# Sixteen ring slots, the first two experts' loads first, and single row buffers in a mixture-of-experts stage on one core

## The chip, the cores and the metric

The kernel runs on one core of a Trainium2 chip. The metric is the device time of one execution in microseconds (us); lower is better. TensorE does the matrix products, VectorE (DVE) and ScalarE (ACT) work on elements, GpSimd (POOL) does small work and issues the row gathers and scatters, and SyncE (SP) issues the weight loads. Sixteen DMA engines move the data for all queues.

## The reference

One layer of a diffusion backbone on 640 tokens (128 context, 512 latent) of 1024 channels, in float32: attention and merge, then a mixture of experts. Only the last part matters here:

```python
D_MODEL, N_GROUPS, EXPERTS_PER_GROUP, TOP_K, D_EXPERT = 1024, 4, 8, 2, 512     # 32 experts
g_sel = argmax(t @ w_router_group + b_router_group)                  # one group of 4 per token
le_sel = (t @ w_router_expert + b_router_expert) of that group       # 8 logits
top_v, top_i = top_k(le_sel, 2)
w_pair = softmax(group logits)[g_sel] * softmax(top_v)
for each expert e: hb = silu(x @ w1[e]) * (x @ w3[e]);  y = (hb @ w2[e]) * weight
channel_sublayer(x) = x + gate * rms_norm(sum of the two experts' y, g_post_ffn)
```

w1 and w3 of an expert are 1024 x 512, w2 is 512 x 1024: 2 MiB each, so that the 32 experts are 192 MiB. A token goes to two experts.

## The kernel before

**Stages.** Projections, attention, merge and the output product take the first 575 us. Then the rows `h2` are normed, stored to a scratch tensor `h2_d` (5 stores of 0.5 MiB on SyncE's queue), and the router follows. Its end is a chain of small VectorE operations: logits, one-hots, positions of each token in its expert's list, the slot table (which token stands in which of an expert's 128 slots: `tab_g` for gathers, `tab_s` for scatters), then the experts' ranks by size and their numbers in that order (`expert_ids`). 

**Passes.** 18 passes process 1, 2 or 4 experts together (`WIDTHS`). The first two (`LEAD`) take experts 0 and 1 by number, the others take experts by rank. A pass gathers its 128 rows by an indirect DMA (`gather`, L968 to L977), TensorE transposes them (`transpose_x`), ScalarE copies the columns, and then come the products with w1 and w3 (`up`), the gate on ScalarE and VectorE, and w2 (`down`). The result is copied to `ysb` (`y_half`) and scattered to `y_d` (`scatter`). Gathered rows (`xg`) and results (`ysb`) have two buffers each, taken in turn. The last pass isn't scattered; its rows are added on chip. At the end five pair loads of 1 MiB bring `y_d` back, and the final rows are made from them and from x1, which stays on chip (`xrow`).

**Units and loads.** `expert_units` cuts each pass into 6 units (w1, w3 and w2 in two halves each). A unit reads one load of 1 MiB for each expert of its pass. The order of units is that of TensorE; the order of loads is that of SyncE. In the prediction a unit or load is called by its number, from 0:

| unit | what | loads before |
|---|---|---|
| 0, 1 | pass 0, w1 | 0, 1 |
| 2, 3 | pass 0, w3 | 2, 3 |
| 4, 5 | pass 1, w1 | 4, 5 |
| 6, 7 | pass 0, w2 | 6, 7 |
| 8, 9 | pass 1, w3 | 8, 9 |
| 10, 11 | pass 2, w1 (two experts) | 10 to 13 |
| 12, 13 | pass 1, w2 | 14, 15 |
| 14, 15 | pass 2, w3 (two experts) | 16 to 19 |
| 16, 17 | pass 3, w1 (four experts) | 20 to 27 |
| 18, 19 | pass 2, w2 (two experts) | 28 to 31 |
| 20, 21 | pass 3, w3 (four experts) | 32 to 39 |

Load j goes to ring slot j % 15. SyncE issues strictly in order, and load j waits for the unit of load j - 15 (`ring_load`, L731 to L742):

```python
if j >= RING:
    sp.wait_ge(moe_mm, moe_loads[j - RING][0] + 1)
```

Loads 0 to 2 go out as the last raw weight slots come free, 3 to 8 as the last split weights do, 9 after the `h2` stores, 10 to 14 after the expert numbers; 13 waits for the first gather as well (L758). Slots 9 to 14 (`rows_ring`) lie where the merged rows and modulation rows were. The order on GpSimd's queue is: gathers 0 and 1, two loads of gate rows, the store of the pair weights, then for each pass the gather two passes on, and the scatter.

Of the kernel before, what the change touches and what calls it, by code (L numbers as in the profile page):

```python
# [7 lines left out]
ALU = mybir.AluOpType  # L8
# [9 lines left out]
P = 128  # L18
# [19 lines left out]
RAW_MIX, RING, HL = 3, 15, 3  # L38
# [70 lines left out]

def build(nc, t):  # L110
# [16 lines left out]
    with ExitStack() as ctx:  # L127
# [32 lines left out]
        h2T = at("h2T", D, offset=att_base + (NT + 6) * D * 4)  # L160
        assert att_base + (NT + 7) * D * 4 <= att_end
# [66 lines left out]
        xg = at("expert_rows", 2 * D, offset=late_base + 2 * D * 4)  # L228
        ysb = at("expert_y", 2 * D, offset=late_base + 4 * D * 4)
        gT = at("expert_g_columns", FE, offset=late_base + 6 * D * 4)  # L230
        g2_rows = at("last_gate_rows", D, offset=late_base + 6 * D * 4 + FE * 4)
# [4 lines left out]
        rows_ring = at("rows_ring", (RING - RAW_MIX - 2 * HL) * UNIT, offset=att_base)  # L236
        assert att_base + (RING - RAW_MIX - 2 * HL) * UNIT * 4 <= att_end
# [28 lines left out]
        rbase = [late_base + 4 * D * 4]  # L266

        def rb(name, cols, dt=F32):
            a = at(name, cols, dt, offset=rbase[0])
            rbase[0] += (cols * (2 if dt == BF16 else 4) + 31) // 32 * 32  # L270
            assert rbase[0] <= late_base + 6 * D * 4
            return a

        kbase = [late_base + 7 * D * 4 + FE * 4]

        def kept(name, cols, dt=F32):
            a = at(name, cols, dt, offset=kbase[0])
            kbase[0] += (cols * (2 if dt == BF16 else 4) + 31) // 32 * 32
            assert kbase[0] <= late_base + 2 * KD * TOK * 4
            return a  # L280
# [50 lines left out]
        def ring(slot):  # L331
# [5 lines left out]
            x = slot - RAW_MIX - 2 * HL  # L337
# [352 lines left out]
        def _(sp):  # L690
# [40 lines left out]
            def ring_load(j):  # L731
# [5 lines left out]
                if p == NP:  # L737
                    if u == 0:
                        sp.wait_ge(all_scattered, 1)
                    load_pair(u)  # L740
# [54 lines left out]
        def _(po):  # L795
# [172 lines left out]
            def gather(p):  # L968
                if p >= 2:
                    po.wait_ge(moe_xt, p - 1)  # L970
# [4 lines left out]
                po.indirect_dma_start(out=xg[:, par * D:(par + 1) * D], out_offset=None, in_=h2_d,  # L975
# [3 lines left out]
            def scatter(p):  # L979
# [5 lines left out]
                                      in_=ysb[:, par * D:(par + 1) * D], in_offset=None,  # L985
# [13 lines left out]
            gather(1)  # L999
# [5 lines left out]
            po.dma_start(wk_d.rearrange("(t p k) o -> p t (k o)", p=P, k=2), wk[:, :].rearrange("p (t k) -> p t k", k=2)).then_inc(g2_in, 16)  # L1005
            for p in range(NP - 1):
# [9 lines left out]
            def later_round(r):  # L1016
                po.wait_ge(tab_done, r + 1)
                with po.Fori(0, NE) as e:
# [4 lines left out]
                    po.indirect_dma_start(out=xg[:, 0:D], out_offset=None, in_=h2_d,  # L1023
# [8 lines left out]
                                          in_=ysb[:, 0:D], in_offset=None,  # L1032
# [19 lines left out]
        def _(ac):  # L1052
# [262 lines left out]
            def y_half(p):  # L1315
                par = p % 2
                ac.wait_ge(moe_mm, unit_end(p, 2, 1))
                if p >= 2:
                    ac.wait_ge(moe_sc[par], 16 * (p // 2))
                ac.activation(ysb[:, par * D:par * D + 512], bank(5), ACT.Copy).then_inc(moe_ya, 1)  # L1320
# [60 lines left out]
        def _(pe):  # L1381
# [345 lines left out]
            ins.then_inc(pre_done, 1)  # L1727

# [15 lines left out]
            pe.wait_ge(ranks_made, 2)  # L1744
            pe.matmul(bank(6)[0:1, 2 * NE:2 * NE + RANKED], tokval[0:NE, 0:1], perm[0:NE, :], start=True, stop=True)
# [15 lines left out]
            xg_v = xg[:, :].rearrange("p (b q k) -> p b k q", b=2, k=KD)  # L1761
            gp_v = gprod[:, :].rearrange("p (q k) -> p k q", k=4)

            def rows_transposed(par):
                for k in range(KD):
                    ins = pe.transpose(bank(k // 4)[:, (k % 4) * P:(k % 4 + 1) * P], xg_v[:, par, k, :], ident[:, :])  # L1766
# [44 lines left out]
            def transpose_x(p):  # L1811
# [3 lines left out]
                rows_transposed(p % 2).then_inc(moe_xt, 1)  # L1815
# [40 lines left out]
            for i in range(NT):  # L1856
# [3 lines left out]
                for x in range(2):  # L1860
                    pe.matmul(bank(SUM_BANK[i] + x), loh[:, i * P:(i + 1) * P], ysb[:, LAST_PAR * D + x * 512:LAST_PAR * D + x * 512 + 512], start=True, stop=False)
                pair_rows(i)

            def later_round(r):
                slot_table(r)
                with pe.Fori(0, NE) as e:
                    n = pe.snap(e + (NE * (r - 1) + 1))
                    pe.wait_ge(moe_g[0], n * 16 + 16 * N_PAR[0])
                    rows_transposed(0).then_inc(moe_xt, 1)
# [29 lines left out]
        def _(ve):  # L1899
# [395 lines left out]
            ve.wait_ge(pre_done, 1)  # L2295
            taken = rtw[:, :].rearrange("p (k n) -> p k n", k=2)
# [11 lines left out]

            slot_table(0, slot_pos)
# [3 lines left out]
            counts = bank(5)[0:NE, NT * NE:(NT + 1) * NE]  # L2313
            on_diag = ident[0:NE, 0:NE]
            key, dg, small = count_key[0:NE, :], diag[0:NE, :], rank_small[0:NE, :]
            rank, size, done = small[:, 1:2], small[:, 2:3], small[:, 3:4]
            link(ve.scalar_tensor_tensor(key, counts, float(NE), order_bias[0:NE, :], ALU.mult, ALU.add))
            link(ve.tensor_tensor(dg, key, on_diag, ALU.mult))
            link(ve.tensor_reduce(small[:, 0:1], dg, AX.X, ALU.add))
            link(ve.tensor_scalar(key, key, small[:, 0:1], None, ALU.is_gt))  # L2320
            link(ve.tensor_reduce(rank, key, AX.X, ALU.add))
            link(ve.tensor_scalar(perm[0:NE, :], iota32[0:NE, 0:RANKED], rank, None, ALU.is_equal))
# [19 lines left out]
            ve.wait_ge(ids_mm, 2)  # L2342
            link(ve.tensor_copy(expert_ids[0:1, :], bank(6)[0:1, 2 * NE:2 * NE + RANKED]))
            ve.tensor_scalar(expert_ids[0:1, :], expert_ids[0:1, :], 1, None, ALU.logical_shift_right).then_inc(ids_done, 1)
# [29 lines left out]
            def y_half(p):  # L2374
                par = p % 2
                ve.wait_ge(moe_mm, unit_end(p, 2, 1))
                if p >= 2:
                    ve.wait_ge(moe_sc[par], 16 * (p // 2))
                ve.tensor_copy(ysb[:, par * D + 512:(par + 1) * D], bank(6)).then_inc(moe_yv, 1)  # L2379
# [109 lines left out]
```

## Time and profile before

| | |
|---|---|
| median of 3 runs | 1144.94 us (1143.33 to 1145.46) |
| profiled execution | 1144.4 us, of which the span from the first to the last instruction 1142.7 us |
| mean granted TensorE clock | 0.959 |
| busy: TensorE products, DVE, ACT, POOL | 1004.3, 355.0, 280.8, 138.3 us |
| DMA | 301.55 MB, mean 264 GB/s |
| weight and pair loads, SyncE's queue | 271.07 MB, 60.5% of 16 engines over the span |

How to read it: busy times are sums of one engine's instructions; matrix products are pipelined, so a busy TensorE isn't one at its peak. A float32 product stands in the trace as two records, so that a unit of one load is 16 records. The DMA share of a stretch is the mean busy share of the 16 DMA engines.

### The profile page before, as it was taken

The numbers are of one execution on the slowest core, as the hardware profiler recorded it, in microseconds if no ns is written. First come the engines' busy times: TensorE is split into PE (matmuls) and PEld (weight loads), VectorE is DVE, ScalarE is ACT, GpSimd is POOL, SyncE is SP. The second block draws the span as 40 slices with busy tenths as digits, with TensorE's granted clock in tenths as the row PEclk, the third lists the DMA queues.
The fourth block names the chain that finished last, engine by engine and source line by source line (L and its number), as shares of the span: only waits on it lengthen the run. The fifth ranks groups of instructions, "written<-read, shape, count | busy, mean of one in ns | idle before, by whom it ended". The sixth has DMA issues, their size and how long they took to land. (4 is left out here: it accounts for less than half of the span.)

```text
span 1142.7 us, 13820 instructions
## 1 busy us (share of the span) xinstructions
PE 1004.3 (88%) x5483; PEld 606.3 (53%) x5483; DVE 355.0 (31%) x633; ACT 280.8 (25%) x533; POOL 138.3 (12%) x219
## 2 busy tenths in 40 slices
PE   4999999999988898999968997799999978588776
PEld 2677778777766787887854332233333322122222
DVE  3553133110388885462392110000000000000006
ACT  4233213222377664022341000000011000000004
POOL 2122221000111301100122000000001000000000
PEclk9899999999989999999997998899999998889999
DMA  9734436444350212633458999999999999999973
GB/s 350 254 113 160 126 110 226 160 168 177 123 184 1 77 55 66 230 129 93 184 202 283 369 401 420 421 422 421 421 420 420 421 419 419 419 416 413 416 312 135
DMA packets 73334, 301.55 MB, mean 264 GB/s; under 512 B 8055, under 2 KB 14328, under 8 KB 48050
## 3 DMA queue, kind: packets, MB, share of 16 engines
q1 hardware_dynamic: 62064, 271.07, 60.5%
q0 software_dynamic: 11040, 29.49, 7.6%
q8 instruction: 46, 0.75, 0.3%
q14 instruction: 22, 0.18, 0.1%
q10 hardware_dynamic: 162, 0.05, 0.0%
HBM read 283.34 MB, written 25.33 MB: 270 GB/s over the span
## 5 line engine op out<-in xcount | busy, mean ns | idle before, releaser
L1387 PE MATMUL psum<-w_hi,act_hi 128*128 128x512 f32 (+1 forms) x480 | 188.6, 393 | 2.8 <-ACT rows L1174 1.4
L1389 PE MATMUL psum<-w_hi,act_lo 128*128 128x512 f32 (+1 forms) x480 | 183.9, 383 | 0.0
L1388 PE MATMUL psum<-w_lo,act_hi 128*128 128x512 f32 (+1 forms) x480 | 183.7, 383 | 0.0
L1782 PE MATMUL psum<-weights_ring,expert_x_columns 128*64 128x512 f32 (+1 forms) x584 | 125.3, 634 | 29.5 <-DMA weights_ring<-in_w_e 18.5
L1320 ACT ACTIVATE expert_y<-psum 128x512 f32<-128x512 f32 x18 | 10.8, 597 | 455.3 <-PE psum L1793 455.3
L1782 PE MATMUL psum<-rows_ring,expert_x_columns 128*64 128x512 f32 (+1 forms) x448 | 103.6, 611 | 9.5 <-DMA rows_ring<-in_w_e 5.9
L1387 PEld LDWEIGHTS psum<-w_hi,act_hi 128*128 128x128 f32 x480 | 90.9, 189 | 32.4 <-issue 14.2
L1389 PEld LDWEIGHTS psum<-w_hi,act_lo 128*128 128x128 f32 x480 | 90.9, 189 | 18.2
L1388 PEld LDWEIGHTS psum<-w_lo,act_hi 128*128 128x128 f32 x480 | 91.1, 190 | 16.3
L1911 DVE TENSOR_TENSOR w_lo<-raw_mix,w_hi 128x2048 fp32r<-128x2048 f32 (+1 forms) x24 | 52.8, 2202 | 148.1 <-ACT w_hi L1069 148.1
L1782 PEld LDWEIGHTS psum<-weights_ring,expert_x_columns 128*64 128x64 f32 (+1 forms) x584 | 37.5, 136 | 103.5 <-issue 102.3
L2379 DVE COPY expert_y<-psum 128x512 f32<-128x512 f32 x18 | 12.4, 691 | 224.8 <-PE psum L1793 224.8
L1793 PE MATMUL psum<-rows_ring,expert_g_columns 128*64 128x512 f32 (+1 forms) x288 | 64.6, 625 | 14.4 <-DMA raw_mix<-in_w_e 9.0
L1782 PE MATMUL psum<-raw_mix,expert_x_columns 128*64 128x512 f32 (+1 forms) x248 | 61.5, 630 | 4.1 <-DMA raw_mix<-in_w_e 3.0
L1782 PEld LDWEIGHTS psum<-rows_ring,expert_x_columns 128*64 128x64 f32 (+1 forms) x448 | 31.0, 134 | 63.4 <-issue 62.2
L984 POOL DMA_INDIRECT y_scratch<-expert_y,pass_scatter_rows x15 | 15.0, 1002 | 392.8 <-PE psum L1766 335.8
L2368 DVE TENSOR_TENSOR gprod<-psum,gsil 128x512 f32<-128x512 f32 x18 | 12.4, 691 | 156.6 <-PE psum L1782 156.6
L1069 ACT ACTIVATE w_hi<-raw_mix 128x2048 fp32r<-128x2048 f32 (+1 forms) x24 | 44.2, 1842 | 65.5 <-PE psum L1389 39.1
L1793 PE MATMUL psum<-weights_ring,expert_g_columns 128*64 128x512 f32 (+1 forms) x208 | 52.7, 618 | 6.1 <-DMA weights_ring<-in_w_e 5.3
L1202 ACT ACTIVATE rows<-psum,soft 128x640 f32<-128x640 f32 (+3 forms) x80 | 50.6, 642 | 4.8 <-DVE soft L2096 2.5
L1793 PEld LDWEIGHTS psum<-rows_ring,expert_g_columns 128*64 128x64 f32 (+1 forms) x288 | 20.3, 134 | 54.9 <-issue 54.9
L1793 PE MATMUL psum<-raw_mix,expert_g_columns 128*64 128x512 f32 (+1 forms) x144 | 41.7, 664 | 8.5 <-DMA weights_ring<-in_w_e 5.9
(345 smaller groups left out, 1275.2 us busy)
## 6 DMA issues: line engine op xcount, KB each, us to landing
weights_ring<-in_w_e SPq DMA_DIRECT2D x78, 1024.0 KB, 28.1
rows_ring<-in_w_e SPq DMA_DIRECT2D x75, 1024.0 KB, 28.5
raw_mix<-in_w_e SPq DMA_DIRECT2D x39, 1024.0 KB, 27.7
raw_mix<-in_w_in SPq DMA_DIRECT2D x16, 1024.0 KB, 5.8
raw_mix<-in_w_ada SPq DMA_DIRECT2D x16, 1024.0 KB, 7.1
ada_first<-in_w_ada SPq DMA_DIRECT2D x8, 1024.0 KB, 14.3
gates_scratch<-rows POOLq DMA_DIRECT2D x20, 256.0 KB, 3.3
y_scratch<-lam SPq DMA_DIRECT2D x1, 5120.0 KB, 16.8
```

The source lines that it names most:

```text
L984: po.indirect_dma_start(out=y_d, out_offset=bass.IndirectOffsetOnAxis(pass_rows(tab_s, pass_s, p), 0), in_=ysb[:, par * D:(par + 1) * D], ...
L1069: ac.activation(whi(s % HL)[:, :, 0:w], raw(n % RAW_MIX)[:, :, 0:w], ACT.Copy).then_inc(hi_done, 1)
L1202: ac.activation(e[:, m * w:(m + 1) * w], s_view(i)[:, m, :], ACT.Exp, bias=soft[:, 16 * b + m:16 * b + m + 1], accum_out=total).then_inc(e ...
L1320: ac.activation(ysb[:, par * D:par * D + 512], bank(5), ACT.Copy).then_inc(moe_ya, 1)
L1387: pe.matmul(out, a_hi(ka_), w_hi[:, kw, :], start=s, stop=False)
L1388: pe.matmul(out, a_hi(ka_), w_lo[:, kw, :], start=False, stop=False)
L1389: ins = pe.matmul(out, a_lo(ka_), w_hi[:, kw, :], start=False, stop=e)
L1782: ins = pe.matmul(out[x * w:(x + 1) * w, :], expert_xT[:, a:a + w], ring(slots[x % len(slots)])[:, kk * 512:(kk + 1) * 512], start=(k == 0 ...
L1793: ins = pe.matmul(bank(5 + b_)[x * w:(x + 1) * w, :], gT[:, k * P + x * w:k * P + (x + 1) * w], ring(slots[x % len(slots)])[:, kk * D + b_ ...
L1911: ve.tensor_tensor(wlo(s % HL)[:, :, 0:w], raw(n % RAW_MIX)[:, :, 0:w], whi(s % HL)[:, :, 0:w].bitcast(F32), ALU.subtract).then_inc(lo_don ...
L2368: ve.tensor_tensor(gprod[:, :], bank(3), gsil[:, :], ALU.mult).then_inc(moe_gp, 1)
L2379: ve.tensor_copy(ysb[:, par * D + 512:(par + 1) * D], bank(6)).then_inc(moe_yv, 1)
```

## The change

- The ring has 16 slots (`RING`). `rows_ring` now has places for seven of them, in the order [9, 0, 6, 7, 8, 5, 4] of ten places that end at `pt`; x1 (`rows`) stays between them. `h2T` moves to the place of `expert_xT`.
- The loads are sorted so that all twelve of passes 0 and 1 come first: loads 10 and 11 are now those of units 12 and 13, 12 to 15 those of units 10 and 11. From 16 on the order is as before. Load j waits for the unit of load j - 16.
- Load 9 goes out with 3 and 4, load 10 after the last split weights, load 11 after the gated halves (`mix_done`), 12 after `h2_part` and the expert numbers, 13 on after the `h2` stores. The waits for the first gather (L758) and for the router (L760) are gone.
- `xg` and `ysb` have one buffer. A gather waits for the transposes of the pass before, the copy of y for the scatter of the pass before. The second gather moves behind the gate rows and the pair weights on GpSimd's queue.
- VectorE makes the ranks (6 operations) and, as soon as TensorE has summed them, the expert numbers (2 operations) before the slot table.
- The five pair loads are issued together after one wait for a unit and `all_scattered`.

```diff
-RAW_MIX, RING, HL = 3, 15, 3
+RAW_MIX, RING, HL = 3, 16, 3
...
     loads = [(n, p, m, u, x) for n, (p, m, u) in enumerate(units) for x in range(len(passes[p]))]
+    loads.sort(key=lambda x: x[1] >= LEAD)
...
-        xg = at("expert_rows", 2 * D, offset=late_base + 2 * D * 4)
-        ysb = at("expert_y", 2 * D, offset=late_base + 4 * D * 4)
+        h2T = at("h2T", D, offset=late_base)
+        xg = at("expert_rows", D, offset=late_base + 2 * D * 4)
+        ysb = at("expert_y", D, offset=late_base + 3 * D * 4)
...
-        rows_ring = at("rows_ring", (RING - RAW_MIX - 2 * HL) * UNIT, offset=att_base)
+        rows_ring_base = pt_base - 10 * UNIT * 4
+        rows_ring = at("rows_ring", 10 * UNIT, offset=rows_ring_base)
...
-            x = slot - RAW_MIX - 2 * HL
+            x = [9, 0, 6, 7, 8, 5, 4][slot - RAW_MIX - 2 * HL]
...
                     ring_load(RAW_MIX + 2 * x + 1)
+                    if x == 0:
+                        ring_load(9)
+                ring_load(10)
+                sp.wait_ge(mix_done, 6 * NT)
+                ring_load(11)
                 for i in range(NT):
                     sp.wait_ge(h2_done, i + 1)
                     sp.dma_start(h2_d[i * P:(i + 1) * P, :], yr[:, i, :]).then_inc(h2_out, 16)
+                sp.wait_ge(h2_part, NT)
+                ring_load(12)
                 sp.wait_ge(h2_out, 16 * NT)
                 sp.wait_ge(h2t_done, 2 * NT)
-                for j in range(RAW_MIX + 2 * HL, len(moe_loads)):
-                    if j == RAW_MIX + 2 * HL + 4:
-                        sp.wait_ge(moe_g[0], 16)
-                    if j == RING - 1:
-                        sp.wait_ge(rt_mm, 1 + NT)
+                for j in range(13, len(moe_loads)):
                     ring_load(j)
...
             def pairs(again):
+                if not again:
+                    sp.wait_ge(moe_mm, moe_loads[PAIR_LOAD + NT - 1 - RING][0] + 1)
+                    sp.wait_ge(all_scattered, 1)
                 for i in range(NT):
-                    if again:
-                        load_pair(i)
+                    load_pair(i)
...
             def gather(p):
-                if p >= 2:
-                    po.wait_ge(moe_xt, p - 1)
+                if p >= 1:
+                    po.wait_ge(moe_xt, p)
...
             gather(0)
-            gather(1)
...
             po.dma_start(wk_d.rearrange("(t p k) o -> p t (k o)", p=P, k=2), wk[:, :].rearrange("p (t k) -> p t k", k=2)).then_inc(g2_in, 16)
+            gather(1)
...
             def y_half(p):
...
-                if p >= 2:
-                    ve.wait_ge(moe_sc[par], 16 * (p // 2))
-                ve.tensor_copy(ysb[:, par * D + 512:(par + 1) * D], bank(6)).then_inc(moe_yv, 1)
+                if p:
+                    ve.wait_ge(moe_sc[1 - par], 16 * ((p + 1) // 2))
+                ve.tensor_copy(ysb[:, 512:D], bank(6)).then_inc(moe_yv, 1)
```

In VectorE's program the lines L2313 to L2322 (ranks) and L2343 and L2344 (numbers) now stand ahead of `slot_table(0, slot_pos)`, with the positions (L2296 to L2298) between them; TensorE's product for the numbers (L1745) moves ahead of its part of the slot table.

## Rows read from the trace of the kernel before

**Rows 1.** The page, rate of all DMA in 40 slices of 28.6 us.
```profile
GB/s 350 254 113 160 126 110 226 160 168 177 123 184 1 77 55 66 230 129 93 184 202 283 369 401 420 421 422 421 421 420 420 421 419 419 419 416 413 416 312 135
```

**Rows 2.** Stretches: us, busy us (instructions) of PE, PEld, DVE, ACT, POOL, granted clock, DMA share, GB/s.
```profile
600.00:605.00 5.00, 3.14 (x30) 2.63 (x30) 3.90 (x21) 0.23 (x1) 1.76 (x2) 0.50 0.07 10
...
640.00:660.00 20.00, 20.00 (x98) 7.38 (x96) 2.07 (x3) 2.10 (x3) 2.06 (x2) 1.00 0.95 342
...
820.00:900.00 80.00, 73.96 (x342) 28.16 (x344) 6.22 (x9) 6.33 (x9) 6.05 (x6) 0.98 1.01 420
```

**Rows 3.** Single issues of L742 on SyncE: duration ns, issue us, then time to landing.
```profile
L742 SPq DMA_DIRECT2D weights_ring<-in_w_e x2: 432/432/432, 553.0 to 553.5; - x2
L742 SPq DMA_DIRECT2D raw_mix<-in_w_e x1: 328/328/328, 552.6 to 552.6; - x1
DMA to landing us min/median/max: 4.9/7.0/9.0
...
L742 SPq DMA_DIRECT2D rows_ring<-in_w_e x2: 332/332/333, 655.4 to 655.9; - x2
DMA to landing us min/median/max: 7.4/8.5/9.6
...
L742 SPq DMA_DIRECT2D raw_mix<-in_w_e x1: 332/332/332, 671.0 to 671.0; - x1
DMA to landing us min/median/max: 8.5/8.5/8.5
```

**Rows 4.** SyncE's timeline: start us, length us, line, transfer; loads 10 to 14 and 15 to 17.
```profile
608.42 3.29 SPq L742 DMA_DIRECT2D rows_ring<-in_w_e  x5
616.46 9.57 SPq L742 DMA_DIRECT2D raw_mix<-in_w_e  x3
```

**Rows 5.** TensorE's timeline: units 0 and 1, transposes, units 12 and 13, transposes, unit 21.
```profile
610.58 9.27 PE L1782 MATMUL psum<-raw_mix,expert_x_columns 128*64 128x512 f32 x32 [1.11 <-ACT expert_x_columns L1307]
...
643.57 1.16 PE L1766 MATMUL psum<-ident,expert_rows 128*128 128x128 f32 x8
...
659.27 3.60 PE L1793 MATMUL psum<-rows_ring,expert_g_columns 128*64 128x512 f32 x16
662.71 3.60 PE L1793 MATMUL psum<-raw_mix,expert_g_columns 128*64 128x512 f32 x16
666.24 1.16 PE L1766 MATMUL psum<-ident,expert_rows 128*128 128x128 f32 x8
...
701.07 1.07 PE L1782 MATMUL psum<-weights_ring,expert_x_columns 128*32 128x512 f32 x3 [7.16 <-DMA rows_ring<-in_w_e]
```

**Rows 6.** VectorE's timeline: first position operation, ranks, and numbers, each with its follower.
```profile
598.28 0.49 DVE L2297 TENSOR_TENSOR route_tmp<-onehots,psum 128x320 f32<-128x320 f32 x1
...
602.04 0.17 DVE L2317 SCALAR_TENSOR_TENSOR count_keys<-psum,order_bias 32x32 f32<-32x32 f32 x1
...
603.40 0.14 DVE L2324 TENSOR_SCALAR rank_small<-rank_small 32x1 f32<-32x1 f32 x1
...
606.63 0.18 DVE L2343 CAST expert_numbers<-psum 1x30 int32<-1x30 f32 x1
...
606.93 0.41 DVE L2346 COPY slot_table_columns<-psum 32x256 f32<-32x256 f32 x1
```

**Rows 7.** Gathers of passes 0 and 2 on GpSimd, each with its time to landing.
```profile
L975 POOL DMA_INDIRECT expert_rows<-h_scratch,gather_rows x1: 1127/1127/1127, 602.9 to 602.9; - x1
DMA to landing us min/median/max: 4.5/4.5/4.5
...
L975 POOL DMA_INDIRECT expert_rows<-h_scratch,pass_gather_rows x1: 1052/1052/1052, 622.3 to 622.3; - x1
DMA to landing us min/median/max: 9.0/9.0/9.0
```

**Rows 8.** Issues over the whole span: transfer, count, KB each, median us to landing.
```profile
rows_ring<-in_w_e SPq DMA_DIRECT2D x75, 1024.0 KB, 28.5
...
expert_rows<-h_scratch,pass_gather_rows POOLq DMA_INDIRECT x16, 10.7
```

More of the change, by code:

```diff
@@ L270, in rb @@
             rbase[0] += (cols * (2 if dt == BF16 else 4) + 31) // 32 * 32
-            assert rbase[0] <= late_base + 6 * D * 4
+            assert rbase[0] <= late_base + 4 * D * 4 + FE * 4
             return a
-        kbase = [late_base + 7 * D * 4 + FE * 4]
+        kbase = [late_base + 5 * D * 4 + FE * 4]
         def kept(name, cols, dt=F32):
@@ L974, in gather @@
                 par = p % 2
-                po.indirect_dma_start(out=xg[:, par * D:(par + 1) * D], out_offset=None, in_=h2_d,
+                po.indirect_dma_start(out=xg[:, :], out_offset=None, in_=h2_d,
                                       in_offset=bass.IndirectOffsetOnAxis(pass_rows(tab_g, pass_g, p), 0),
@@ L1022, in later_round @@
                     po.sem_inc(row_dmas, 1)
-                    po.indirect_dma_start(out=xg[:, 0:D], out_offset=None, in_=h2_d,
+                    po.indirect_dma_start(out=xg[:, :], out_offset=None, in_=h2_d,
                                           in_offset=bass.IndirectOffsetOnAxis(idx_g[:, 0:1], 0),
@@ L1727, in _ @@
             ins.then_inc(pre_done, 1)
+            pe.wait_ge(ranks_made, 2)
+            pe.matmul(bank(6)[0:1, 2 * NE:2 * NE + RANKED], tokval[0:NE, 0:1], perm[0:NE, :], start=True, stop=True).then_inc(ids_mm, 1)
             def slot_table(r):
@@ L1742, in _ @@
             ins.then_inc(tabt_mm, 1)
-            pe.wait_ge(ranks_made, 2)
-            pe.matmul(bank(6)[0:1, 2 * NE:2 * NE + RANKED], tokval[0:NE, 0:1], perm[0:NE, :], start=True, stop=True)
+            pe.wait_ge(ranks_made, 3)
             pe.matmul(bank(6)[:, 0:2 * NE], ones_row[0:NE, :], excess[0:NE, :], start=True, stop=True).then_inc(ids_mm, 1)
@@ L1860, in _ @@
                 for x in range(2):
-                    pe.matmul(bank(SUM_BANK[i] + x), loh[:, i * P:(i + 1) * P], ysb[:, LAST_PAR * D + x * 512:LAST_PAR * D + x * 512 + 512], start=True, stop=False)
+                    pe.matmul(bank(SUM_BANK[i] + x), loh[:, i * P:(i + 1) * P], ysb[:, x * 512:x * 512 + 512], start=True, stop=False)
                 pair_rows(i)
@@ L2295, in _ @@
             ve.wait_ge(pre_done, 1)
+            counts = bank(5)[0:NE, NT * NE:(NT + 1) * NE]
+            on_diag = ident[0:NE, 0:NE]
+            key, dg, small = count_key[0:NE, :], diag[0:NE, :], rank_small[0:NE, :]
+            rank, size, done = small[:, 1:2], small[:, 2:3], small[:, 3:4]
+            link(ve.scalar_tensor_tensor(key, counts, float(NE), order_bias[0:NE, :], ALU.mult, ALU.add))
+            link(ve.tensor_tensor(dg, key, on_diag, ALU.mult))
+            link(ve.tensor_reduce(small[:, 0:1], dg, AX.X, ALU.add))
+            link(ve.tensor_scalar(key, key, small[:, 0:1], None, ALU.is_gt))
+            link(ve.tensor_reduce(rank, key, AX.X, ALU.add))
+            ve.tensor_scalar(perm[0:NE, :], iota32[0:NE, 0:RANKED], rank, None, ALU.is_equal).then_inc(ranks_made, 1)
             taken = rtw[:, :].rearrange("p (k n) -> p k n", k=2)
@@ L2307, in slot_table @@
                 ve.tensor_scalar(tab_g[:, :], tab_s[:, :], 1, None, ALU.logical_shift_right).then_inc(tab_done, 1)
+            ve.wait_ge(ids_mm, 2)
+            link(ve.tensor_copy(expert_ids[0:1, :], bank(6)[0:1, 2 * NE:2 * NE + RANKED]))
+            ve.tensor_scalar(expert_ids[0:1, :], expert_ids[0:1, :], 1, None, ALU.logical_shift_right).then_inc(ids_done, 1)
             slot_table(0, slot_pos)
             ve.tensor_tensor(E3[:, :, 4:5], s5(4).unsqueeze(2), s5(2).unsqueeze(2), ALU.subtract).then_inc(r_exp_in, 1)
[L2313 to L2322, printed above, removed]
             link(ve.tensor_scalar(done, rank, float(ALONE), 64.0, ALU.is_lt, ALU.mult))
```

39 lines of the change are left out of this document (16 added, 23 removed).

## The prediction

> **What bounds the kernel now.** I read the slices of the page first [rows 1]. The reader is to see a rate of about 420 GB/s held from slice 25 nearly to the end: the 192 expert loads of 1 MiB. The stretches confirm it [rows 2]: in 820 to 900 us the DMA engines are full (share 1.01, 420 GB/s), TensorE is busy 74 of 80 us; a load takes 28.5 us from issue to landing there [rows 8]. One MiB at 420 GB/s is 2.5 us, so some eleven loads are queued and a load lands every 2.5 us. In that regime the end comes 2.5 us later for each load by which the queue is behind, whatever TensorE does.
>
> So the question is where the load list stands when it goes over into that regime. Before it, two things hold the list back. In 600 to 605 us the DMA engines are almost idle (10 GB/s): load 10 waits for the expert numbers and leaves at 608.42 us [rows 2, 4]. Then the ring is full: load 15 goes out at 616.46, when unit 0 is done [rows 4]. Experts 0 and 1 cost TensorE 3.4 us per unit of one load (units 12 and 13 start 3.44 us apart [rows 5]), longer than the 2.5 us of the load, so the DMA catches up with TensorE and waits for slots: 640 to 660 us shows 342 GB/s instead of 420 [rows 2]. Loads 25 and 26 leave together at 655.4 us when unit 10 is done and land after 7.4 and 9.6 us, at 662.8 and 665.5; load 31 leaves at 671.0 and lands at 679.5 [rows 3]. From here on units take two to four loads each, and the queue stays full. TensorE meets its first long wait for a load at 701 us (7.16 us, unit 21) [rows 5]. The landing of load 31, 679.5 us, is my mark: what moves it moves the end by as much.
>
> **The change, part by part.** *Earlier loads.* Loads 9, 10 and 11 go out at the last products and at the gated halves, 12 to 15 when the numbers are there. All sixteen land before or around unit 0, five more than have landed at 618 us before (load 10 left at 608.42 with the queues of the gather and the gate rows ahead). By itself that is 5 x 2.5 = 12.5 us of stream. But the ring then is full at once, and load 16 waits for unit 0, 17 for unit 1: the DMA gets one load per 3.4 us and more, and has no backlog in the whole stage of experts 0 and 1. Earlier landing of loads whose units cannot start is worth nothing. What stays is one slot: each wait names a unit one load earlier.
>
> *Order of loads.* Here the same edit takes more than the slot gives. After the sort, ring positions 10 and 11 hold loads of units 12 and 13 (the down products of expert 1), and 12 to 15 those of units 10 and 11. Loads are issued in order, so 26 waits for unit 12, 27 for unit 13, and 28 to 31, whose slots are long free, stand behind 27. Before, 25 and 26 went at unit 10, 27 and 28 at unit 11, 29 at unit 12, 30 at unit 13. After it, between unit 9 and unit 12 nothing is issued, and since there is no backlog the DMA really pauses. Unit 12 ends at 662.9 and unit 13 at 666.3 us [rows 5]. Let S be the time by which TensorE's experts start later. Load 27 goes at 666.3 + S. On an empty queue the first load lands after 4.9 us and the next ones 2 to 2.5 us apart (4.9, 7.0, 9.0 for the three at 552.6 us [rows 3]). So load 31 lands at 666.3 + S + 4.9 + 4 x 2.5 = 681.2 + S. To it comes what the scatter and the gather between the passes take: before, loads 26 to 31 needed 679.5 - 665.5 = 14.0 us instead of 12.5 [rows 3], so 1.5 us. Sum 682.7 + S, against 679.5: **3.2 + S**. Bounds: 2.0 apart instead of 2.5 and no scatter, 3.5 us less (the stream then is 0.3 us early); a scatter and a gather in full (1 MiB, 2.5 us), 1 us more.
>
> *Ranks and numbers first.* The six rank operations, 602.04 to 603.40, move ahead of the slot table: 1.36 us; so do the two that make the numbers, 606.63 to 606.93: 0.30 us [rows 6]. TensorE's small product for the numbers runs while VectorE does the two position operations of 0.5 us each that start at 598.28 now [rows 6], so that wait costs nothing; without this cover it would be 0.3 to 0.5 us. The slot table, and with it the first gather, is 1.7 us late. The numbers come at 598.3 + 1.4 + 1.0 + 0.3 = 601.0 us instead of 606.9, and with the 1.5 us from there to SyncE's first issue [rows 4, 6] load 12 leaves at 602.5 instead of 608.4. It saves nothing, by the paragraph on loads.
>
> *The first gather among loads.* Now it starts at 602.9 and lands after 4.5 us, with both queues empty (the load that comes next waits for the numbers until 608.4) [rows 4, 7]. After the change it starts at 604.6 us, when loads 12 to 15 have just been issued (five such issues take 3.3 us [rows 4]): 4 MiB or 10 us of queue. The gather at 622.3 us, with such a backlog of loads, took 9.0 us [rows 7]; the median over the later passes is 10.7 [rows 8]. I take 9.0: 4.5 us more. Everything of the experts hangs on it: transposes, columns, unit 0 at 610.58 [rows 5]. Bounds: 4.5 (no cost) and 10.7 (6.2 us more). The wait for the first gather that load 13 had before is gone, so nothing protects it. In sum S = 1.7 + 4.5 = **6.2 us**, with bounds of 1.7 and 7.9.
>
> The Trainium skill (DMA: Bandwidth & Descriptors, Queues, rings and completion order) says that each DMA engine goes round between the queues packet by packet. By that the gather shares the engines instead of standing behind 10 us of loads, and the sum would be that of rival (a); the row of 9.0 us, beside loads as well, does not agree.
>
> *Single buffers.* The gather for a pass now needs the transposes of the pass before. TensorE transposes at the start of each pass, 22.7 us apart (643.57 and 666.24 [rows 5]), a gather lands in 10.7 [rows 8]: hidden, with 12 us to spare. The second gather is the exception: it moves from behind the first to behind two gate row loads, the pair weights and the first transposes, that is to about 1 us before unit 0, 615.7 us. It is needed after units 0 and 1, 9.3 us of products and 1.2 of small ones after 616.8 [rows 5]: at 627.1. With 9.0 it lands at 624.7. Hidden, with 2.4 us to spare; with 10.7, 0.7. In its place on GpSimd's queue stand the next gather, the last slot's weights and the scatter of pass 0, which is 20 us off. The y copies wait for the scatter of the pass before, one pass earlier: hidden in the same way. The pair loads wait for the last scatter as before. h2's stores go behind loads 10 and 11 on SyncE's queue, but the gather waits 10 us longer for its table than for them. Cost nothing. The clear of the row buffer halves, hidden.
>
> **Sum.** 3.2 + 6.2 = 9.4 us. The profiled execution took 1144.4 us, so 1153.8 us (span 1152.1). The median of the runs is 1144.94, 0.5 above it, and the runs lie 2.1 apart; I leave the figure as it is.
>
> **Rivals.**
> *(a) The gather shares the engines.* It takes turns with the loads; at half of 420 GB/s its 0.5 MiB take 2.5 us instead of 1.25, so it lands in 4.5 to 5.8. For it: loads 12 to 15 are out only 0 to 2 us before it. Against it: 9.0 and 10.7 in the rows. Then S is 1.7 to 3.0: 1149.3 to 1150.6 us. This is what the round of the Trainium skill (same section) would give.
> *(b) The second gather is late.* If both gathers take 10.7 or more, with the gate rows between, TensorE waits at the second transposes and units 2 on are later by 1 to 3 us: with S at 7.9 the sum is 12 to 14, 1156 to 1158 us. The Trainium skill (Trainium Kernel Development and Optimization, Best Practices) advises double buffers; this is the place where giving one up would show.
> *(c) Faster: the lead of the loads survives.* If the DMA still has a backlog when unit 9 ends, the hold of loads 26 to 31 is covered, and S too; then the stream keeps the slot and perhaps more: 2.5 us at least, 1141.9, and 12.5 at most, 1132. It decides at the rate of slots against landings: fewer than 2.5 us per unit of one load, against 3.44 in the rows, and 342 GB/s in 640 to 660 speaks against a backlog even with loads issued late.
> *(d) No change.* S near its low bound and the loads closely spaced: 3.2 - 3.5 + 1.7 = 1.4 us, 1145.8.
>
> **Chances.** My forecast 0.60, (a) 0.16, (b) 0.10, (c) 0.09, (d) 0.05. A change of under 0.2% (2.3 us) can't be told from none with this kernel. Faster is (c), 0.09; same is (d), 0.05; slower the rest, 0.86. The range goes from 1147 (below (a), for a cheaper restart of the loads) to 1158 (all of (b)); it leaves out (c), (d) and little more.
>
> **What the profile after would show.** Slot table 1.7 us later; load 12 issued near 602.5; the first gather about 9 us to landing, unit 0 at 616.8; 640 to 665 us under 330 GB/s; a gap of about 11 us between the issues of loads 25 and 26 and then five in a row near 672.5; load 31 landing near 689, and from 710 us the same 420 GB/s as before, all landings 9 us late, the ending unchanged. If the first gather takes 5 us, (a); if GB/s stays at 420 through 650 to 675, the step on the order is wrong, and with it the sign. I would also be wrong if the stream were not bound by the DMA all the way, so that TensorE made up what the loads lost.

## The result: slower by 11.6 us, and the profile after

The changed kernel takes 1155.95 us (1154.48 to 1157.64 in 4 runs), against 1144.38 (1143.33 to 1145.46 in 4 runs) of the kernel before: a ratio of 1.0106, 95% interval 1.0094 to 1.0119, so 11.6 us slower. The profiled execution took 1154.48 us, its span is 1152.7.

The page of the changed kernel, rate of all DMA in 40 slices of 28.8 us:

```profile
GB/s 355 244 133 165 116 100 215 191 177 171 119 147 1 93 55 121 173 137 64 241 249 280 291 306 420 420 421 420 421 420 421 420 420 420 418 419 413 417 316 133
```

Beside [rows 1], slices 23 and 24 (634 to 692 us) fall from 369 and 401 to 291 and 306. That is where bytes are missing; from slice 25 on nothing differs. The stretches tell it apart; columns as in [rows 2]:

```profile
600.00:605.00 5.00, 3.79 (x32) 3.13 (x32) 3.96 (x20) 0.23 (x1) 1.80 (x3) 0.50 0.58 177
605.00:610.00 5.00, 0.03 (x1) 0.00 (x0) 1.88 (x7) 0.00 (x0) 1.33 (x2) 0.50 1.02 425
640.00:660.00 20.00, 20.00 (x98) 7.01 (x94) 1.38 (x2) 2.10 (x3) 2.07 (x2) 1.00 0.88 307
660.00:670.00 10.00, 10.00 (x50) 3.73 (x50) 0.69 (x1) 0.00 (x0) 0.00 (x0) 1.00 0.24 72
820.00:900.00 80.00, 73.94 (x350) 27.49 (x346) 6.92 (x10) 6.33 (x9) 6.04 (x6) 1.00 1.02 421
```

Two of these stretches of the kernel before are not in [rows 2]:

```profile
605.00:610.00 5.00, 2.84 (x12) 2.15 (x12) 3.38 (x15) 0.50 (x1) 2.41 (x4) 0.50 0.94 254
660.00:670.00 10.00, 10.00 (x52) 3.79 (x50) 2.49 (x8) 2.10 (x3) 1.83 (x2) 1.00 0.97 385
```

The idle DMA of 600 to 605 us is filled (177 GB/s for 10). From 605 to 610 TensorE stands still (busy 0.03 us, before 2.84) while the DMA runs at 425 GB/s (before 254). In 660 to 670 us TensorE is fully busy in both kernels, and the DMA moves 72 GB/s for 385, a sixth of what it moves with a full queue. In 820 to 900 us the rate is that of before.

SyncE's timeline (start, length, line, transfer) for loads 12 to 15, 16 to 18 and 25 to 31, after [rows 4]:

```profile
601.15 2.60 SPq L741 DMA_DIRECT2D rows_ring<-in_w_e  x4
...
621.51 9.56 SPq L741 DMA_DIRECT2D raw_mix<-in_w_e  x3
...
656.98 17.81 SPq L741 DMA_DIRECT2D rows_ring<-in_w_e  x7
```

The group of seven takes 17.81 us, because there is a hole in it. The single issues of loads 25, 26 and 31, each with its time to landing, after [rows 3]:

```profile
L741 SPq DMA_DIRECT2D rows_ring<-in_w_e x1: 332/332/332, 657.0 to 657.0; - x1
DMA to landing us min/median/max: 7.2/7.2/7.2
...
L741 SPq DMA_DIRECT2D rows_ring<-in_w_e x1: 333/333/333, 668.1 to 668.1; - x1
DMA to landing us min/median/max: 4.8/4.8/4.8
...
L741 SPq DMA_DIRECT2D rows_ring<-in_w_e x1: 400/400/400, 674.4 to 674.4; - x1
DMA to landing us min/median/max: 14.6/14.6/14.6
```

Load 25 lands at 664.2 us, load 26 leaves at 668.1 and lands after 4.8 us, the time of a load on an empty queue (4.9 in [rows 3]). So no load was in flight in between. Load 31 lands at 674.4 + 14.6 = 689.0, against 679.5.

TensorE's timeline, after [rows 5]: the first transposes, units 0 and 1, the second transposes, units 12 and 13 (in one group), and the transposes of pass 3. In brackets stands the idle time before and what ended it:

```profile
612.36 1.97 PE L1771 MATMUL psum<-ident,expert_rows 128*128 128x128 f32 x8 [7.32 <-DMA expert_rows<-h_scratch,gather_rows]
...
615.44 9.46 PE L1787 MATMUL psum<-raw_mix,expert_x_columns 128*64 128x512 f32 x32 [1.11 <-ACT expert_x_columns L1311]
...
625.96 1.16 PE L1771 MATMUL psum<-ident,expert_rows 128*128 128x128 f32 x8
...
664.33 7.04 PE L1798 MATMUL psum<-rows_ring,expert_g_columns 128*64 128x512 f32 x32
671.30 1.16 PE L1771 MATMUL psum<-ident,expert_rows 128*128 128x128 f32 x8
```

VectorE's timeline, after [rows 6]: the last rank operation, the first position operation, the numbers, and the last of the slot table.

```profile
598.12 0.23 DVE L2310 TENSOR_SCALAR rank_onehot<-iota,rank_small 32x30 f32<-32x30 f32 x1
598.27 0.47 DVE L2312 TENSOR_TENSOR route_tmp<-onehots,psum 128x320 f32<-128x320 f32 x1
...
599.29 0.18 DVE L2325 CAST expert_numbers<-psum 1x30 int32<-1x30 f32 x1
...
602.13 0.18 DVE L2322 TENSOR_SCALAR gather_rows<-scatter_rows 128x32 uint32<-128x32 uint32 x1
```

And the first gather, after [rows 7]:

```profile
L979 POOL DMA_INDIRECT expert_rows<-h_scratch,gather_rows x1: 1126/1126/1126, 603.2 to 603.2; - x1
DMA to landing us min/median/max: 9.1/9.1/9.1
```

**Where the 11.6 us are.** The stages ahead of the experts end a few microseconds earlier or later from run to run, whatever the kernel: load 0 leaves at 503.7 us in the profile before, at 502.5 after, at 508.3 in a second profile of the changed kernel. So I count from that issue. The table holds this for all kernels whose records are complete; load 31 is the 32nd load to land.

| kernel | first gather, +landing | unit 0 starts | load 31 lands | last load lands | end of span |
|---|---|---|---|---|---|
| before | 99.2 +4.5 | 106.8 | 175.8 | 605.7 | 638.9 |
| after | 100.7 +9.1 | 113.0 | 186.6 | 616.7 | 650.2 |
| after_again | 100.7 +9.8 | 113.7 | 187.0 | 617.3 | 650.9 |
| order_renamed | 100.7 +9.6 | 113.4 | 178.2 | 609.7 | 642.9 |
| gather_first | 100.7 +4.5 | 108.4 | 182.2 | 612.4 | 645.6 |
| ranks_late | 99.3 +4.6 | 107.0 | 180.9 | 610.9 | 644.1 |
| renamed_ranks_late | 99.2 +4.6 | 107.0 | 172.6 | 604.4 | 637.6 |
| late_fill | 99.2 +4.5 | 106.8 | 172.3 | 603.6 | 636.8 |
| fifteen_slots | 99.3 +4.6 | 106.9 | 176.6 | 606.8 | 640.3 |
| before_single | 99.2 +4.6 | 106.9 | 177.2 | 606.7 | 640.1 |

After less before: unit 0 +6.2, load 31 +10.8, last load +11.0, end +11.3. Nearly all of it arises ahead of load 31, and the stream carries it to the end with 0.5 us more.

### The profile page after: what moved, and what is told of

Read it like the earlier page. It is cut to its first block and busy times, and to the rows that moved or that the text cites. A ratio compares the mean times of both kernels' runs of the same rounds, so it can differ in the third digit from the quotient of the medians.

```text
span 1152.7 us, 13826 instructions
## 1 busy us (share of the span) xinstructions
PE 1002.6 (87%) x5483; PEld 604.9 (52%) x5483; DVE 354.5 (31%) x633; ACT 280.9 (24%) x533; POOL 137.5 (12%) x219
## 5 line engine op out<-in xcount | busy, mean ns | idle before, releaser
L1787 PE MATMUL psum<-rows_ring,expert_x_columns 128*64 128x512 f32 (+1 forms) x520 | 117.7, 619 | 20.3 <-DMA rows_ring<-in_w_e 20.3
L1324 ACT ACTIVATE expert_y<-psum 128x512 f32<-128x512 f32 x18 | 10.8, 597 | 460.0 <-PE psum L1798 460.0
L1798 PE MATMUL psum<-rows_ring,expert_g_columns 128*64 128x512 f32 (+1 forms) x320 | 73.0, 604 | 10.9 <-DMA raw_mix<-in_w_e 6.2
L1787 PE MATMUL psum<-raw_mix,expert_x_columns 128*64 128x512 f32 (+1 forms) x272 | 71.5, 664 | 11.7 <-DMA weights_ring<-in_w_e 8.0
L1787 PEld LDWEIGHTS psum<-rows_ring,expert_x_columns 128*64 128x64 f32 (+1 forms) x520 | 35.9, 136 | 79.3 <-issue 78.1
L1798 PE MATMUL psum<-weights_ring,expert_g_columns 128*64 128x512 f32 (+1 forms) x248 | 64.1, 643 | 14.8 <-DMA weights_ring<-in_w_e 12.2
L2374 DVE TENSOR_TENSOR gprod<-psum,gsil 128x512 f32<-128x512 f32 x18 | 12.5, 692 | 162.6 <-PE psum L1787 162.6
L1798 PEld LDWEIGHTS psum<-rows_ring,expert_g_columns 128*64 128x64 f32 (+1 forms) x320 | 24.2, 134 | 52.5 <-issue 51.5
L1787 PEld LDWEIGHTS psum<-raw_mix,expert_x_columns 128*64 128x64 f32 (+1 forms) x272 | 21.2, 145 | 54.1 <-issue 51.7
## 6 DMA issues: line engine op xcount, KB each, us to landing
rows_ring<-in_w_e SPq DMA_DIRECT2D x84, 1024.0 KB, 28.5
```

Of the source, the lines that this page charges most:

```text
L1324: ac.activation(ysb[:, 0:512], bank(5), ACT.Copy).then_inc(moe_ya, 1)
L1787: ins = pe.matmul(out[x * w:(x + 1) * w, :], expert_xT[:, a:a + w], ring(slots[x % len(slots)])[:, kk * 512:(kk + 1) * 512], start=(k == 0 ...
L1798: ins = pe.matmul(bank(5 + b_)[x * w:(x + 1) * w, :], gT[:, k * P + x * w:k * P + (x + 1) * w], ring(slots[x % len(slots)])[:, kk * D + b_ ...
L2374: ve.tensor_tensor(gprod[:, :], bank(3), gsil[:, :], ALU.mult).then_inc(moe_gp, 1)
```

## The experiments

Times are medians. Every ratio is against the kernel before, run on the same chip in the same session (its medians: 1144.2, 1143.56 and 1143.63 us in the three sessions). My theory had two causes, independent of each other: the *hold* (loads 26 to 31 wait for units 12 and 13, by the sort) and the *late start* (first gather later and among loads, by the ranks and numbers ahead of the slot table).

**after_again**, the changed kernel unchanged, as a yardstick.

> The changed kernel once more, as the reference of this group on the same chip. Both theories: 11 to 12 us over the kernel before (1155 to 1157 us), load 12 near 601, first gather 9 us to landing, a gap of 11 us between the issues of loads 25 and 26.

1157.69 us (1153.96 to 1161.0), ratio 1.0108 (1.0084 to 1.0132). The profile has the gather at 9.8 us, and by the table the same losses. It is the profile of the longest of the six executions, 1161.0 us, and its load 0 leaves 5.9 us later than after: that excess arises ahead of the experts.

**order_renamed** takes away the hold alone: no sort; loads 14 and 15 (of units 12 and 13) go out early in place of 10 and 11, so as much is loaded ahead as in the changed kernel, but each later load waits for the next unit in order.

```diff
-    loads.sort(key=lambda x: x[1] >= LEAD)
...
-            x = [9, 0, 6, 7, 8, 5, 4][slot - RAW_MIX - 2 * HL]
+            x = [9, 7, 8, 5, 4, 0, 6][slot - RAW_MIX - 2 * HL]
...
-                ring_load(10)
+                ring_load(14)
...
-                ring_load(11)
+                ring_load(15)
...
-                ring_load(12)
+                ring_load(10)
...
-                for j in range(13, len(moe_loads)):
+                for j in [11, 12, 13] + list(range(16, len(moe_loads))):
```

> Same loads at the same times in the same places, but the six loads of units 10 to 13 get ring positions in the order of their units, so that loads 26 to 31 wait for units 10, 10, 11, 11, 12, 13. My theory (the hold of loads 26 to 31 costs about half of the loss): 7 to 8 us under the changed kernel, about 1148 us; no gap over 6 us between issues after load 15, load 31 lands near 682. Rival 1 (the late start of unit 0 is the whole loss): under 2 us. Rival 2 (the single row buffers cost it): no change.

1147.5 us (1145.41 to 1149.43), ratio 1.0025 (1.0013 to 1.0037). Its stretches:

```profile
640.00:660.00 20.00, 20.00 (x100) 7.54 (x100) 2.06 (x3) 2.10 (x3) 2.06 (x2) 1.00 0.88 294
660.00:670.00 10.00, 10.00 (x50) 3.60 (x48) 0.71 (x2) 0.00 (x0) 0.00 (x0) 1.00 0.97 356
670.00:680.00 10.00, 10.00 (x50) 3.75 (x48) 2.49 (x8) 2.10 (x3) 2.02 (x2) 1.00 0.98 388
```

660 to 670 us has 356 GB/s where the changed kernel had 72. In the table load 31 lands 8.4 us earlier than after and the end comes 7.3 us earlier, while unit 0 is as late as after (113.4). So the pause of the loads comes from the order, and it costs 7 to 8 us by itself. The loads' rate in 640 to 660 us is as low as after: that is the stage in which TensorE sets the pace, in both.

**gather_first** takes away only the loads ahead of the first gather: load 12 waits for it.

```diff
+                sp.wait_ge(moe_g[0], 16)
                 ring_load(12)
```

> Load 12 waits for the landing of the first gather; nothing else. My theory (the gather is slow because four loads are in front of it, and early loads 12 to 15 are worth nothing): the gather lands in 4.5 us instead of 9, unit 0 starts 4.5 us earlier, loads 12 to 15 go out near 608, and the kernel is 4 to 5 us faster than the changed one, about 1151.5 us. Rival 1 (four loads on their way early are worth their 10 us of stream): slower than the changed kernel by 2 us or more. Rival 2 (the gather is slow for another reason): gather 9 us, no gain.

In the trace it did what was expected: the gather lands in 4.5 us, unit 0, load 31 and the end are all 4.4 to 4.6 us earlier than after. The times are less clear: 1153.66 us (1150.59 to 1159.05), ratio 1.0098 (1.0074 to 1.0121), whose interval overlaps that of after_again. As a time this run is inconclusive; the profile, a single execution, carries it.

**ranks_late** takes away the whole late start: ranks and numbers behind the slot table again, as before, in VectorE's program and in TensorE's.

```diff
-            link(ve.scalar_tensor_tensor(key, counts, float(NE), order_bias[0:NE, :], ALU.mult, ALU.add))
...
-            ve.tensor_scalar(perm[0:NE, :], iota32[0:NE, 0:RANKED], rank, None, ALU.is_equal).then_inc(ranks_made, 1)
...
             slot_table(0, slot_pos)
...
+            link(ve.scalar_tensor_tensor(key, counts, float(NE), order_bias[0:NE, :], ALU.mult, ALU.add))
...
+            ve.tensor_scalar(perm[0:NE, :], iota32[0:NE, 0:RANKED], rank, None, ALU.is_equal).then_inc(ranks_made, 1)
```

> The ranks and numbers are made after the slot table again, as in the kernel before; all else as changed. My theory: slot table 1.7 us earlier, and the loads that need the numbers leave 6 us later, so that the gather is alone and lands in 4.5 us: unit 0 starts 6 us earlier, 6 us faster than the changed kernel, about 1149.5 us, still 5 us over the kernel before by the hold. Rival 1 (early loads are worth having): slower than the changed kernel. Rival 2 (only the 1.7 us of VectorE count): 1.7 us faster.

1149.44 us (1149.03 to 1155.31), ratio 1.0063 (1.0039 to 1.0087). By the table the first gather starts 1.4 us earlier than after and lands in 4.6, and unit 0 starts at 107.0, as before. With it load 31 is 5.7 and the end 6.1 us earlier. So the late start costs about 6 us by itself. The intervals of the two ratios just touch, and it is again the trace that gives the size. One new thing is seen on TensorE's timeline, at the second transposes:

```profile
621.00 1.16 PE L1771 MATMUL psum<-ident,expert_rows 128*128 128x128 f32 x8 [0.58 <-DMA expert_rows<-h_scratch,gather_rows]
```

The second gather is now waited for. I come back to it below.

**renamed_ranks_late** has both repairs.

> Both repairs together: ring positions of the six loads in the order of their units, and ranks and numbers after the slot table. My theory (hold and late start add up, and what is left is one slot more): 2.5 us under the kernel before, 1141.5 to 1142.5 us, unit 0 within 0.3 us of before, load 31 lands 3 us earlier than before. What speaks against it: in the two kernels with an early start the second gather took 11 us and landed as TensorE needed it; if that counts, 0.5 to 1 us of the gain are gone. Rival (sixteen slots give nothing where the queue is full anyway): the time of the kernel before.

1142.31 us (1141.36 to 1145.21), ratio 0.9991 (0.998 to 1.0002). That is 1.25 us under the kernel before, half of the 2.5 us expected, and not clear of no change. The two by two:

| | late start | start as before |
|---|---|---|
| hold | 1155.95, 1157.69 | 1149.44 |
| no hold | 1147.5 | 1142.31 |

Counted in the traces, at the end of the span: 650.2 and 650.9 with both, 642.9, 644.1 and 637.6. The hold costs 7.3 to 8.0 us beside the late start and 6.5 without it; the late start costs 6.1 to 6.8 beside the hold and 5.3 without it. Together they cost 12.6 to 13.3, and they are all that made the change slower: without them it is 1.3 us ahead of before in the traces. That agrees with what is left of it, by the runs below: a slot, 2.7 us to the good, and single buffers, 1.2 to the bad.

**fifteen_slots**: renamed_ranks_late with one slot fewer, to price the slot.

```diff
-RAW_MIX, RING, HL = 3, 16, 3
+RAW_MIX, RING, HL = 3, 15, 3
...
-                ring_load(15)
...
-                for j in [11, 12, 13] + list(range(16, len(moe_loads))):
+                for j in [11, 12, 13] + list(range(15, len(moe_loads))):
```

> The kernel with both repairs, with 15 slots instead of 16; load 15 then goes when unit 0 is done. My theory (a slot is worth one load of the stream): 2.5 us slower than with 16, and so within 1 us of the kernel before, though loads 9 and 14 go out 30 us earlier than there and the row buffers are single. Rival: no difference between 15 and 16.

1145.09 us (1142.28 to 1147.27), ratio 1.0008 (0.9996 to 1.0021): 2.8 us above renamed_ranks_late in the medians of twelve runs each, 2.7 in the traces, though the intervals of the two ratios overlap a little. A slot is worth one load's time, 2.5 us by the rate, and little more.

**late_fill**: renamed_ranks_late, but loads 14 and 15 are issued in their turn after the expert numbers, 33 to 36 us later.

```diff
-                ring_load(14)
-                sp.wait_ge(mix_done, 6 * NT)
-                ring_load(15)
...
-                for j in [11, 12, 13] + list(range(16, len(moe_loads))):
+                for j in list(range(11, len(moe_loads))):
```

> The kernel with both repairs, but the two loads of expert 1's down products (positions 14 and 15) are issued after the numbers, behind 10 to 13, some 30 us later. My theory (loads landed before their slots' units can start are worth nothing, since TensorE sets the pace there): within 1 us of the kernel with both repairs. Rival (an early load is 2.5 us of stream): 5 us slower.

1142.11 us (1141.02 to 1146.93), ratio 0.9991 (0.9976 to 1.0006), the same as renamed_ranks_late to 0.2 us in the medians; in the traces the end is 0.8 us earlier. Loads that go out early for units that can't start are worth nothing here.

**before_single**: the kernel before, with the single row buffers of the change, the second gather's place on GpSimd's queue that they need, and nothing else of it.

```diff
-                if p >= 2:
-                    po.wait_ge(moe_xt, p - 1)
+                if p >= 1:
+                    po.wait_ge(moe_xt, p)
...
-                po.indirect_dma_start(out=xg[:, par * D:(par + 1) * D], out_offset=None, in_=h2_d,
+                po.indirect_dma_start(out=xg[:, 0:D], out_offset=None, in_=h2_d,
...
-            gather(1)
...
+            gather(1)
...
-                if p >= 2:
-                    ve.wait_ge(moe_sc[par], 16 * (p // 2))
-                ve.tensor_copy(ysb[:, par * D + 512:(par + 1) * D], bank(6)).then_inc(moe_yv, 1)
+                if p:
+                    ve.wait_ge(moe_sc[1 - par], 16 * ((p + 1) // 2))
+                ve.tensor_copy(ysb[:, 512:D], bank(6)).then_inc(moe_yv, 1)
```

> The kernel before with single buffers for gathered rows and for y, and the second gather behind the gate rows, the pair weights and the first transposes; nothing else. My theory: the later passes hide it; the second gather lands 0 to 1 us late among loads 10 to 14, so 0 to 1 us slower. Rival (single buffers are part of the loss): 3 us or more.

1145.27 us (1143.09 to 1147.14), ratio 1.0013 (1.0002 to 1.0025): 1.7 us slower in the medians, 1.2 in the traces, a little over the 0 to 1 expected. The profile shows the second gather issued right into the loads 10 to 14, landing late, and TensorE's wait for it:

```profile
L975 POOL DMA_INDIRECT expert_rows<-h_scratch,gather_rows x1: 1059/1059/1059, 608.6 to 608.6; - x1
DMA to landing us min/median/max: 11.4/11.4/11.4
```

```profile
620.11 1.16 PE L1766 MATMUL psum<-ident,expert_rows 128*128 128x128 f32 x8 [0.96 <-DMA expert_rows<-h_scratch,gather_rows]
```

The transposes of all later passes show no wait for their gather. So single buffers cost about 1 us where the second gather is issued among loads, and it is the second gather that costs it.

**second_gather_early**: renamed_ranks_late, with the second gather right behind the first, into a part of `expert_xT` that isn't used yet, so that it is ahead of the loads without a second row buffer.

```diff
+            link(po.memset(expert_xT[:, D:2 * D], 0.0))
...
-                if p >= 1:
-                    po.wait_ge(moe_xt, p)
+                if p >= 2:
+                    po.wait_ge(moe_xt, p if p > 2 else 1)
...
-                po.indirect_dma_start(out=xg[:, :], out_offset=None, in_=h2_d,
+                po.indirect_dma_start(out=expert_xT[:, D:2 * D] if p == 1 else xg[:, :], out_offset=None, in_=h2_d,
...
+            gather(1)
...
-            gather(1)
...
-                rows_transposed().then_inc(moe_xt, 1)
+                rows_transposed(xg1_v if p == 1 else None).then_inc(moe_xt, 1)
```

> The kernel with both repairs, and the second gather right behind the first, into the place where ScalarE later puts that pass's columns. My theory: it lands in 5 us, TensorE's wait of 1.0 us before the second transposes is gone and every unit of the stage that TensorE paces is 0.5 to 1 us earlier: 0.5 to 1 us faster than the kernel with both repairs, 1141 to 1142 us, 2 us under the kernel before. Rival: no change, since the DMA and not TensorE sets load 31.

1141.57 us (1138.97 to 1147.15), ratio 0.9981 (0.9968 to 0.9994): 2.1 us faster than the kernel before. The wait is gone from TensorE's timeline:

```profile
618.76 1.16 PE L1773 MATMUL psum<-ident,expert_x_columns 128*128 128x128 f32 x8
```

The difference to renamed_ranks_late is not one that these times resolve, since the intervals overlap. In the trace the span ends 636.6 us after load 0, 1.0 us earlier than there; the table leaves the kernel out because the landings of most of its loads are missing from the trace.

**one_load_ahead** and **two_loads_ahead** are the changed kernel with the loads after 12, or after 13, waiting for the first gather. The diff is that of the first; the second has 14 in place of 13. They measure what a gather pays for loads queued ahead of it.

```diff
                 for j in range(13, len(moe_loads)):
+                    if j == 13:
+                        sp.wait_ge(moe_g[0], 16)
                     ring_load(j)
```

> The changed kernel, where loads 13 and on wait for the landing of the first gather, so that one load of 1 MiB is ahead of it instead of four. If the gather shares the engines with what is queued while it moves: 5 to 6 us to landing. If any load in the queues costs the full price: 9 us.

> The same with two loads ahead. Sharing theory: 6.5 to 8 us to landing, the second load 1 us late. If any load costs the full price: 9 us.

The first gather of one_load_ahead, then of two_loads_ahead:

```profile
L981 POOL DMA_INDIRECT expert_rows<-h_scratch,gather_rows x1: 1127/1127/1127, 602.8 to 602.8; - x1
DMA to landing us min/median/max: 4.7/4.7/4.7
```

```profile
L981 POOL DMA_INDIRECT expert_rows<-h_scratch,gather_rows x1: 1127/1127/1127, 604.5 to 604.5; - x1
DMA to landing us min/median/max: 7.2/7.2/7.2
```

With one load ahead (issued 2.0 us earlier) the gather pays 0.2 us, less than I expected; with two it pays 2.7. One execution of each took 1150.31 and 1153.16 us; in the traces the ends are 646.5 and 647.6 us after load 0, against 650.2 after.

## Why the prediction was right

The forecast was 1153.8 us in a range of 1147 to 1158; measured are 1155.95. Sign, mechanism and place of both terms hold, and the sum is 2 us short. The profiled execution is closer, 1154.48 us, and load 31 lands at 689.0 as forecast (near 689), but in part by luck: this whole execution is 1.3 us early. Counted from load 0 the sum of 9.4 us stands against 10.8 at load 31 and 11.3 at the end.

**S, 6.2 us forecast, 6.2 measured** (unit 0, 106.8 to 113.0 in the table). Its two parts: the first gather starts 1.5 us later (forecast 1.7) and lands in 9.1 us instead of 4.5 (forecast 9.0). Load 12 was to leave at 602.5; it left at 601.15, nearly all of it because this whole run was 1.3 us early, and it was worth nothing, as said: late_fill and ranks_late, in which loads go out later, lose nothing by it.

**The hold, forecast "3.2 + S" at load 31, measured 4.6 + 6.2.** This is the term that was mis-sized, by 1.4 us. The gap between the issues of loads 25 and 26 is 11.1 us (forecast about 11), and load 27 leaves at 671.5 us, which counted from load 0 is 0.2 later than I put it (169.0 for 162.6 + 6.2). What was too small is the burst behind it: from the issue of load 27 to the landing of load 31 I had 4.9 + 4 x 2.5 + 1.5 = 16.4 us, and it took 17.5. I took the 1.5 us for the scatter and the gather between the loads from a stretch of before. No run takes the missing 1.1 us apart. That the hold is the order and not the ring's size or the late start is shown by order_renamed: 356 GB/s for 72, and 7.3 to 8.0 us back with the late start and the sixteen slots kept. The forecast of the hold by itself was 3.2 + 2.5 for the slot, 5.7; the traces say 6.5 to 8.0 at the end and 8.3 to 8.8 at load 31.

**The slot** was taken at one load's time, 2.5 us; fifteen_slots gives 2.8 in the medians and 2.7 in the traces.

**The stream carries it.** Last load +11.0, end +11.3 for load 31 +10.8. TensorE made up nothing of it, so load 31's landing was a fair mark. In the kernels without the hold it is less so: renamed_ranks_late is 3.2 us ahead of before at load 31 and 1.3 at the end.

**The rivals.** *(a)* fell: the gather lands in 9.1 us, not 4.5 to 5.8. Its time holds in one_load_ahead only (4.7); already two loads ahead make 7.2. Its mechanism, both queues served at once, is in the trace, at another price (see below). *(b)* did not come to pass in the changed kernel: the second gather, issued at 615.1, landed in 6.4 us, 4 us ahead of its transposes at 625.96, which show no wait. It was hidden behind the late start. In the six kernels whose first gather lands in 4.5 or 4.6 us and whose second stands behind the gate rows it does: 11.1 to 11.6 us to landing and 0.6 to 1.3 us of waiting (before_single, ranks_late and gather_first among them). The mechanism was right; I had tied it to the wrong condition, slow gathers after a late start. What it needs is that the second gather is issued together with the loads that wait for the numbers or for the first gather, four to six of them. Two sums in the prediction are off, without weight: the second gather is needed at 627.3 us (616.8 + 9.3 + 1.2), not 627.1, and (b) by its own terms reaches 1158.5, not 1158. *(c)* fell by 72 GB/s in 660 to 670 us: there was no backlog when unit 9 ended. Its slot was there, as fifteen_slots shows, and the hold took more. *(d)* fell with S.

**Turns between queues, and double buffers.** That the DMA engines go round between queues (Trainium skill, DMA: Bandwidth & Descriptors, Queues, rings and completion order) gave rival (a) its time, and the gather's 9.1 us doesn't bear that time out: the loads add 4.6 us, where an even share adds 1.3 at most. Yet the gather with eleven loads queued, 28.5 us deep [rows 8], takes 10.7, so it doesn't stand behind them either. The packets show where the 4.6 us are. Here is what each queue moved after the issue of the gather at 603.2 us (q1 is SyncE's queue, q0 GpSimd's; packets, MB, share of the 16 engines), first in 603.2 to 607.5 us, then in 607.6 to 611.9:

```profile
q1 hardware_dynamic: 231, 1.76, 99.0%
...
q1 hardware_dynamic: 181, 1.25, 69.1%
q0 software_dynamic: 175, 0.54, 30.9%
```

For 4.4 us nothing of GpSimd's queue moves; in the kernel before its first packet comes 1.8 us after the issue. That is 2.5 us. From the first packet to the landing it is 4.8 us for 2.7, as both queues now move side by side and GpSimd's gets 30% of the bytes, not half: 2.1 us more. So the trace agrees in that both queues are served at the same time once the gather moves, and what rival (a) missed is the late first packet and the smaller share. The Trainium skill's advice of double buffers (Trainium Kernel Development and Optimization, Best Practices) is worth 1.2 us in the kernel before, and nothing in the changed one, where no transposes wait for a gather but the first.

## What to carry to other kernels

Where one queue issues strictly in order and every load waits for the slot's last reader, the order in which slots come free must be the order of the loads: sorting the first round by who needs it changes the second round's waits, and one slot freed late holds every load behind it. Fill the queue late rather than ahead of a small transfer on which the next stage hangs; a load that lands long before its reader buys nothing while the path runs through that small one. When both a gain and a loss are at work, price each alone (here a slot 2.7 us, the order 6.5 to 8, the late start 5.3 to 6.8) before judging the whole.

## What was unexpected of the hardware

The time of a gather of at most 0.5 MiB against the 1 MiB loads issued around it: 4.5 us with none, 4.7 with one, 7.2 with two, 9.1 to 9.8 with four (after, after_again, order_renamed), and only 10.7 in the steady stream, with eleven loads queued [rows 8]. The second gather takes 11.1 to 11.6 among four to six loads (before_single, ranks_late, gather_first and others), but there the gate rows and the pair weights are ahead of it on its own queue as well, and no run separates the two. Loads right behind a gather can count like those ahead: in gather_first the second one leaves at 611.2 us, loads 12 and 13 at 609.8 and 611.1, 14 and 15 at 611.6 and 612.1, and it takes 11.1.

The step between one and two loads is in the start: the first packet of GpSimd's queue comes 1.8 us after the issue with no load, 1.9 with one, 4.4 with two and with four. From there to the landing it takes 2.7 to 2.8 us with up to two loads, which by then are nearly done, and 4.8 to 5.4 with four. What in the DMA engines holds the first packet back, and why there is a ceiling near 11 us, no run here settles.

A DMA share near 1 doesn't mean a full rate: in 640 to 660 us the share was 0.88 at 294 (order_renamed) and 307 GB/s (after) and 0.95 at 342 (before, [rows 2]), in 660 to 670 us 0.97 at 356 (order_renamed), against 1.01 at 420 in the steady stream. The rate, not the share, showed where the loads were held.
